# Six taps of a 31-tap depthwise convolution on GpSimd, and the down projection's weight loads written out on SyncE

## The reference, cut to what matters

```python
def causal_dwconv(x, w, b):            # one filter per channel, looking back in time
    k, c = w.shape
    y = lax.conv_general_dilated(x, w[:, None, :], (1,), [(k - 1, 0)], ..., feature_group_count=c)
    return y + b

def conformer_conv(x, pw1_w, pw1_b, dw_w, dw_b, ln_g, ln_b, pw2_w, pw2_b):   # dw_w: 31 x 1024
    h = jax.nn.glu(x @ pw1_w + pw1_b, axis=-1)          # 512 tokens x 1024 channels
    h = causal_dwconv(h, dw_w, dw_b)                    # 31 taps
    h = jax.nn.silu(layer_norm(h, ln_g, ln_b))
    return h @ pw2_w + pw2_b

def conv_ffn(x, up_w, conv_w, conv_b, down_w):          # hidden width 2816 = 22 tiles of 128
    gt, val = jnp.split(causal_dwconv(x @ up_w, conv_w, conv_b), 2, axis=-1)
    return (jax.nn.silu(gt) * val) @ down_w
# layer 0: ssd_mixer, conv_ffn; layer 1: conformer_conv, conv_ffn; then a third block with 64 experts
```

## Time and profile before

| | |
|---|---|
| median of 3 runs | 2897.99 us (2888.57 to 2899.99) |
| the profiled execution's own time | 2899.33 us |
| its span | 2897.6 us |
| mean granted clock of TensorE | 0.973 of full |
| busy: PE, DVE, ACT, POOL | 2689.7, 1994.0, 1389.5, 230.2 us |
| layer 0 `conv_ffn`: the down projection begins | 765 us from the start |
| convolution over the 8 tiles | 928 to 1072 us |
| layer 1 `conv_ffn`: the down projection begins | 1398 us |
| third block, from its projections on | about 1510 us to the end |

### The profile page before, as it was taken

One profiled execution on the slowest core, in us unless ns is written; L12 is line 12 of the kernel. 1 busy time (PEld: TensorE's weight loads), 2 busy tenths in 40 slices (PEclk: granted clock), 3 DMA queues, 4 the chain that ended last, 5 costly groups with the idle time before them and its releaser, 6 DMA issues.

```text
span 2897.6 us, 35998 instructions
## 1 busy us (share of the span) xinstructions
PE 2689.7 (93%) x12289; PEld 2048.6 (71%) x12289; DVE 1994.0 (69%) x3046; ACT 1389.5 (48%) x2137; POOL 230.2 (8%) x207
## 2 busy tenths in 40 slices
PE   7999899999997998999998988999899999999995
PEld 6777778788786866888786765586557777777762
DVE  4677644677635975777537545465459999989986
ACT  4666543222324555222324332444448777777772
POOL 0000000000000000000003500000012222222210
PEclk9999999999999999999999998999999999999998
DMA  3222222223232114222233560322259999999996
GB/s 104 67 65 58 73 81 87 87 87 98 78 88 77 52 58 62 87 87 87 80 109 96 153 120 15 116 88 92 105 192 360 337 346 343 342 342 340 339 349 259
DMA packets 317007, 435.09 MB, mean 150 GB/s; under 512 B 45276, under 2 KB 198948, under 8 KB 316644
## 3 DMA queue, kind: packets, MB, share of 16 engines
q1 hardware_dynamic: 299139, 395.61, 42.2%
q0 software_dynamic: 17760, 38.06, 4.4%
HBM read 416.33 MB, written 42.43 MB: 158 GB/s over the span
## 4 chain that ended last, share of the span: by engine, by line
PE 64%; SPq 19%; DVE 7%; ACT 3%; issue 3%; DMA 2%; DVEq 0%; ACTq 0%
PE tp L1263 41%; SPq L943 12%; SPq L950 7%; PE tp L1222 4%; PE tp L1316 1%; PE tp L1317 1%; PE tp L1318 1%; PE tp L1712 1%; DMA sq<-ytab 1%; PE mp L1504 1%; PE mp L1503 1%; PE mp L1505 1%; PE mp L1282 1%; PE mp L1696 1%; PE mp L1676 1%
## 5 line engine op out<-in xcount | busy, mean ns | idle before, releaser
L1263 PE MATMUL tp<-sq_r,arena_r 128*128 128x512 f32 x1152 | 463.6, 402 | 38.7 <-DVE uT_r L2689 25.3
L1263 PE MATMUL tp<-sq_r,wring_r 128*128 128x512 f32 x1152 | 459.3, 399 | 0.0
L1263 PE MATMUL tp<-uT_r,arena_r 128*128 128x512 f32 x1152 | 457.9, 398 | 0.0
L1263 PEld LDWEIGHTS tp<-sq_r,arena_r 128*128 128x128 f32 x1152 | 218.5, 190 | 99.7 <-issue 45.1
L1263 PEld LDWEIGHTS tp<-uT_r,arena_r 128*128 128x128 f32 x1152 | 218.7, 190 | 54.5 <-issue 1.9
L1263 PEld LDWEIGHTS tp<-sq_r,wring_r 128*128 128x128 f32 x1152 | 218.4, 190 | 53.1
L2676 DVE TENSOR_TENSOR wring_r<-wring,arena_r 128x2048 fp32r<-128x2048 f32 x82 | 187.0, 2321 | 62.7 <-ACT arena_r L2021 62.6
L1263 PE MATMUL tp<-arena_r,wring_r 128*128 128x512 f32 x564 | 222.7, 395 | 0.0
L2021 ACT ACTIVATE arena_r<-wring 128x2048 fp32r<-128x2048 f32 x82 | 152.3, 1906 | 34.8 <-DMA wring<-in_a_out_proj 10.8
L2252 ACT ACTIVATE arena<-arena 128x512 f32<-128x512 f32 x44 | 27.8, 633 | 291.0 <-DVE arena L2757 290.9
L3563 DVE TENSOR_TENSOR arena_r<-arena,arena_r 128x1024 fp32r<-128x1024 f32 x128 | 150.4, 1216 | 0.5 <-ACT arena_r L2590 0.5
(11 more groups left out here) (568 smaller groups left out, 6015.2 us busy)
## 6 DMA issues: line engine op xcount, KB each, us to landing
arena<-in_w_exp_down SPq DMA_DIRECT2D x64, 1024.0 KB, 17.4
wring<-in_w_exp_gu SPq DMA_DIRECT2D x64, 768.0 KB, 9.9
uT<-in_w_exp_gu SPq DMA_DIRECT2D x32, 768.0 KB, 9.7
sq<-in_w_exp_gu SPq DMA_DIRECT2D x32, 768.0 KB, 10.3
wring<-in_f_up_w SPq DMA_DIRECT2D x22, 1024.0 KB, 5.2
wring<-in_f_up_w SPq DMA_DIRECT2D x44, 512.0 KB, 6.8
wring<-in_w_exp_gu SPq DMA_DIRECT2D x32, 512.0 KB, 16.7
wring<-in_f_down_w SPq DMA_DIRECT2D x32, 448.0 KB, 5.5
```

The source lines that it names most:

```text
L1263: ins = nc.tensor.matmul(b[:], parts[wp][:, kk, m * P:(m + 1) * P], xparts[xp][:, kk, :], start=n_k == 0 and q == 0, stop=n_k == k - 1 and ...
```

## The change

GpSimd makes six taps of tiles 0 to 6 and four of tile 7, as a product and, from the second on, an addition each, every one waiting for the one before it (`link`). Its sum goes to `pool_part`, and `add_taps` adds it with one more DVE instruction, behind a wait for `pool_taps`. PE makes 8 taps (14 in tile 7) in place of 11 (16), DVE 17 (13) in place of 20 (15). The semaphore behind `pool_taps` is one that a later stage counts on from where it stands, so that stage's base rises by 8. In `ffn` on SyncE the loop over the down projection's slots is replaced by eight calls of `slot`; nothing else calls `loop` but the up projection.

```diff
--- before.py
+++ after.py
@@ -339,8 +339,13 @@
         hglo = [carve_r(HGW) for _ in range(2)]
         tapc_hi = carve_r(CONF_TAPS * NK)
         tapc_lo = carve(CONF_TAPS * NK)
+        top[0] = NBANK * T + NK * HGW + 4 * T + 2 * NK * T + 2 * T + 2 * HGW
+        pool_part = [carve(T) for _ in range(2)]
+        pool_product = acc[3]
         assert top[0] <= ARENA - NSLOT * SLOT
-        PE_TAPS = [11] * (NK - 1) + [16]
+        PE_TAPS = [8] * (NK - 1) + [14]
+        POOL_TAPS = [6] * (NK - 1) + [4]
+        DVE_TAPS = [CONF_TAPS - a - b for a, b in zip(PE_TAPS, POOL_TAPS)]
 
 
         top[0] = NBANK * T
@@ -634,7 +639,7 @@
         SINCE = {"key_turned": 8, "key_spread": 2, "s5_a": 1, "s5_cat": 1, "s5_pow": 3, "s5_bd": 2,
                  "s5_turn": 24, "s5_ct": 8, "s5_bv": 8, "s5_vt": 24, "s5_ca": 8, "s5_km": 8,
                  "s5_kp": 16, "s5_phase": 16, "s5_sin": 32, "s5_mag": 32, "s5_v": 32, "s5_rot": 27,
-                 "s5_x": 18, "s5_yd": 16, "s5_yev": 32,
+                 "s5_x": 18, "s5_yd": 16 + NK, "s5_yev": 32,
                  "tok_out": 16 * 7, "y_out": 16 * 5, "uc_in": 16 * len(par.rows)}
         y_out, uc_in = misc_in, param_in
         key_turned = un_ready
@@ -657,6 +662,7 @@
         s5_rot = ssd["st"]
         s5_x = ssd["y_out"]
         s5_yd = ssd["y"]
+        pool_taps = ssd["y"]
         s5_yev = ssd["ea"]
 
         def runs(ks):
@@ -784,10 +790,8 @@
                 loop(5, 2, 8, body)
                 slot(4, two_cols(up, 10 * 256, FFN + 10 * 256, 256))
 
-                def body2(i):
-                    for j in range(2):
-                        slot(1, thirds(down, FFN_TILES, (2 * i + j) * P, P))
-                loop(4, 2, 2, body2)
+                for m in range(NK):
+                    slot(1, thirds(down, FFN_TILES, m * P, P))
 
             ffn(0)
             for s in range(4):
@@ -1057,6 +1061,18 @@
             for r in raw:
                 nc.gpsimd.memset(r[:, 0:PAD], 0.0)
             pool.drain().then_inc(consts_ready, 1)
+            for j in range(NK):
+                part = pool_part[j % 2]
+                pool.wait_ge(glu_ready, 2 + FFN_TILES + j + 1)
+                if j >= 2:
+                    pool.wait_ge(conv_taken, j - 1)
+                for t in range(DVE_TAPS[j], DVE_TAPS[j] + POOL_TAPS[j]):
+                    x = hg[:, j, CONF_TAPS - 1 - t:CONF_TAPS - 1 - t + T]
+                    w = pc("dw_w", (CONF_TAPS - 1 - t) * NK + j)
+                    link(nc.gpsimd.tensor_tensor(part if t == DVE_TAPS[j] else pool_product, x, w.broadcast_to([P, T]), ALU.mult))
+                    if t > DVE_TAPS[j]:
+                        link(nc.gpsimd.tensor_tensor(part, part, pool_product, ALU.add))
+                pool.nop().then_inc(pool_taps, 1)
             for _ in range(2):
                 phase_end(pool, "pool", ph)
 
@@ -3036,6 +3052,8 @@
 
                 dve.wait_ge(tap_used, sum(PE_TAPS[:j + 1]))
                 link(V.tensor_tensor(cv[:, j, :], cv[:, j, :], cvb[j % 2], ALU.add))
+                dve.wait_ge(pool_taps, 16 + j + 1)
+                link(V.tensor_tensor(cv[:, j, :], cv[:, j, :], pool_part[j % 2], ALU.add))
                 V.tensor_tensor(cv[:, j, :], cv[:, j, :], mp[2 + j % 2][:], ALU.add).then_inc(conv_taken, 1)
 
             for j in range(NK):
@@ -3044,7 +3062,7 @@
                 V.tensor_tensor(hg[:, j, CONF_TAPS - 1:], glu_a[j % 2][:], glu_b[j % 2][:], ALU.mult).then_inc(glu_ready, 1)
                 nglu.inc()
                 dve.wait_ge(glu_ready, 2 + nglu.v)
-                for t in range(CONF_TAPS - PE_TAPS[j]):
+                for t in range(DVE_TAPS[j]):
                     part = cv[:, j, :] if t % 2 == 0 else cvb[j % 2]
                     x = hg[:, j, CONF_TAPS - 1 - t:CONF_TAPS - 1 - t + T]
                     w = pc("dw_w", (CONF_TAPS - 1 - t) * NK + j)
```

## The result

The changed kernel takes 2924.66 us (2920.57 to 2928.21, 4 runs), before 2898.67 us in the same comparison: ratio 1.0097, 95% interval 1.0069 to 1.0124. It is slower by about 26 us. The forecast was 2936 us, from the profiled execution of before; the profiled execution of after took 2927.01 us (span 2925.3). Two effects of opposite sign are in it, as forecast, and the profile shows each.

What follows compares the result with a forecast made beforehand. PE was taken to bound the convolution, with VectorE only 13.6 us shorter, and late weight loads the down projections' heads. 2899.3 + 53.3 (convolution) - 16.6 (loads) = 2936 us; range 2900 to 2965 us.

Steps and rivals of the forecast that it cites:

- VectorE's own work, 120.4 us: Convolution: VectorE's work without waits, 130.2 us, less 15.4 for 23 taps, plus 5.6 for eight additions; about 14.2 us a tile.
- What the two do to each other, 73 us: Convolution: GpSimd's 84 instructions each hold VectorE up, 0.83 us a product and 1.03 an addition; 77 us less 4.
- The doubt that a tap with a per-partition weight might shut out less than a plain product: Convolution: rival in which such products cost VectorE half the loss, giving 2900 us; chance 0.09.
- The first rival, no cost: Convolution: GpSimd runs beside VectorE without cost and PE stays the bound, giving 2867 us; chance 0.08.
- Full exclusion: Convolution: rival in which none of GpSimd's 106 us overlaps VectorE's 120.4; +86 us, 2969 us; chance 0.08.
- The page's rule: Convolution: two-SBUF-input VectorE and SBUF-reading GpSimd instructions exclude each other for a whole instruction; taken literally, 2969 us.
- The wait for PE in tile 7, 3.7 us: End of the convolution: VectorE waits 3.7 us at the last `add_taps`, PE's 14 taps starting at half clock.
- The break-even: Whole change: gain turns to loss where GpSimd costs VectorE more than about 29 us, 0.35 us an instruction.
- The loads, 16.6 us: Heads of both down projections: first load issued 16.7 us earlier, PE's idle time and half clock go; 8.5 and 8.1 us gained.

Runs made afterwards that it cites:

- no_pool_work: Changed kernel with GpSimd's 11 instructions a tile replaced by one zero fill, its taps left out of the result; 2861.54 us, ratio 0.9899 to before.
- pool_writes_only: Changed kernel with GpSimd's products and additions replaced by 22 zero fills a tile (14 in tile 7), which read nothing; 2856.16 us, ratio 0.9881 to before.
- three_pool_taps: Changed kernel with GpSimd making 3 taps a tile (2 in tile 7), PE 11 (16), 38 GpSimd instructions instead of 84; 2893.68 us, ratio 1.0011 to before.
- loads_only: Kernel before with only the down projection's loads written out as eight calls of `slot`, convolution unchanged; 2876.96 us, ratio 0.9950 to before.
- taps_only: Changed kernel with the down projection's load loop put back, so only the taps move to GpSimd; 2939.07 us, ratio 1.0169 to before.
- psum_sum: Changed kernel with VectorE summing its taps as one chain in a PSUM bank instead of two in SBUF; 2873.89 us, ratio 0.9939 to before.
- loads_rebalanced: Kernel before with loads written out, no GpSimd work, PE making 10 taps (14 in tile 7) instead of 11 (16); 2874.06 us, ratio 0.9941 to before.

## Why the prediction was right

The forecast was 2936 us, +36.7 on the profiled execution; +27.7 came, inside the range. By its steps:

- *VectorE's own work, 120.4 us.* Confirmed where it can be seen alone: beside no GpSimd work a plain tile takes 14.48 us (no_pool_work, 947.42 to 961.90 us), against 14.2; the 0.28 us more are the one product that the fill holds up.
- *What the two do to each other, 73 us.* Measured 193.3 - 1.9 - 120.4 = 71 us, 0.85 us each. The pairs came 1.45 and 1.68 us apart at 512 elements; I had 1.50 and 1.70 from the rows at 576 and 1024. The doubt that a tap with a per-partition weight might shut out less than a plain product was unfounded. The reason given, both inputs in SBUF, does not cover VectorE's two plain products at the head of a tile: they read one tensor and lose 0.8 us each as well. The sum had priced them like the rest, and that this came out right is luck. POOL was busy 117.7 us longer than before, not 130. The first rival, no cost, would have been 2867 us; no_pool_work and pool_writes_only show that its number was right for a GpSimd that reads nothing. Full exclusion, with nothing overlapped, was too dear: 86 us against 49.5.
- *The page's rule.* The Trainium skill's page "SBUF — State Buffer" (section "Who interferes with whom") says that a VectorE instruction with two SBUF inputs contends with a GpSimd instruction that reads SBUF, and not with one that only writes. Both halves are borne out here: taps take 1.6 us beside GpSimd's products and additions, 0.67 beside its fills, and with one input in PSUM they stay at 0.79. The same section lets `tensor_scalar` contend as well, by another way; L3073 and L3075, held up even by fills, agree. The page's section "Summary: rules for kernel authors" has the second to issue blocked until the first has finished. For GpSimd's one-input instruction the measurement differs and decides: 1.6 us long, it costs VectorE 0.3.
- *The wait for PE in tile 7, 3.7 us.* 1.9 us came. I had PE run at half clock for 14 matmuls, as in the earlier trace rows; it was 7, and then the full pace:

```profile
1096.61 0.80 PE L1519 MATMUL mp<-arena_r 128*128 128x512 f32 x1 [14.75 <-DVE arena_r L3082]
...
1099.34 0.62 PE L1519 MATMUL mp<-arena_r 128*128 128x512 f32 x1
1099.77 0.43 PE L1520 MATMUL mp<-arena_r 128*128 128x512 f32 x1
1100.03 0.39 PE L1521 MATMUL mp<-arena_r 128*128 128x512 f32 x1
```

- *The break-even.* The prediction put it at about 29 us of cost, 0.35 us an instruction. Its own numbers give more: 143.8 + 16.6 - 120.4 - 3.7 = 36 us, 0.43 each. three_pool_taps, with a cost of 33.9 us and a wait of 5.5, came out 3.4 us above the kernel before.
- *The loads, 16.6 us.* 8.7 + 9.2 = 17.9 us in the two traces, 14.6 us by the medians of loads_only. The mechanism was as described.
- The difference of 9 us between forecast and result is 3.8 in the convolution, 1.3 in the loads, and 3.4 that no step speaks of: 2.0 ahead of the first down projection, 1.4 in the third block, whose length differs from execution to execution (1468 us in taps_only, 1477 in psum_sum, from the end of layer 1's `first_down`).

## What to carry to other kernels

Elementwise work given to GpSimd is not free because GpSimd is idle and has the time: where both it and VectorE read two operands from SBUF they take turns, and a GpSimd instruction that replaces part of a VectorE tap can cost VectorE more (0.85 us) than the tap itself (0.67 us). A tap needs nearly two of them: the 46 taps on GpSimd cost VectorE 71 us, 1.5 us each. Look for rows where the two already ran side by side, and price the pair; if the work is still wanted there, try one of VectorE's operands in PSUM, and compare with a division that leaves GpSimd out: here psum_sum and loads_rebalanced came out alike. And when a loop is written for its first iteration's wait, check what that wait asks for at the entry: here one constant made SyncE sit for three tiles.

## What the runs showed that I had not expected

- GpSimd's one-input products with a constant take 1.49 us for 512 elements while VectorE stands still (1.59 beside its taps), more than its two-input instructions alone (1.04 for a product, 1.30 for an addition), but hold VectorE up by only 0.3 us each.
- GpSimd's fills, which read nothing, still held up VectorE's plain products with one SBUF input and an SBUF output (0.55 to 0.83 us), and were held up by them (0.69 instead of 0.53 us).
- After an idle time of 14.75 us PE ran at half clock (1.2 GHz, granted 0.50) for 3.2 us, after 5.65 us of idle time in the kernel before for 6.1: the longer wait was not followed by the longer slow stretch.
